# All norms of a two-block transformer kernel: split sums spread by two products, 16 columns inverted between block transposes

## The reference

```python
def rms_norm(x, g):
    xf = x.astype(jnp.float32)
    y = xf * lax.rsqrt(jnp.mean(xf * xf, axis=-1, keepdims=True) + NORM_EPS)
    return (y * g.astype(jnp.float32)).astype(x.dtype)
...
def first_block(...):
        xn = rms_norm(h, mix_norm[l])
        proj = jnp.einsum("bsd,dp->bsp", xn, w_in[l]) + b_in[l]
        ...
        hn = rms_norm(h, ffn_norm[l])
        ...
    return rms_norm(h, final_norm)
...
def hybrid_layer(x, norm_gain, w_in, w_out, rel_bias, cos, sin):
    hn = rms_norm_2(x, norm_gain)
    proj = hn @ w_in.astype(hn.dtype)
```

## Time and profile before

| | |
|---|---|
| median of three runs | 1179.32 us (1178.95 to 1179.41) |
| the profiled execution, its own time | 1178.76 us |
| its span | 1177.0 us |
| PE busy | 1169.8 us, 99% |
| DVE busy | 722.0 us, 61% |
| ACT busy | 538.1 us, 46% |
| POOL busy | 149.7 us, 13% |
| mean granted clock of PE | 0.998 |

### The profile page before, as it was taken

How to read it: one execution, slowest core, us unless ns; L and a number is a source line. 1 busy time by engine, 2 the same in 40 slices (tenths; PEclk the granted TensorE clock), 3 DMA queues, 4 the chain that set the end, 5 groups by cost and what they waited for, 6 DMA issues and landing times.

```text
span 1177.0 us, 15915 instructions
## 1 busy us (share of the span) xinstructions
PE 1169.8 (99%) x5704; PEld 964.7 (82%) x5704; DVE 722.0 (61%) x1230; ACT 538.1 (46%) x957; POOL 149.7 (13%) x143
## 2 busy tenths in 40 slices
PE   9999999999999999999999999999999999999997
PEld 8888888888888888888888887788888887788886
DVE  6655884564677777776752635866555445775554
ACT  5522671544444344443241434573664415664653
POOL 4000111002000000000010200256002121263000
PEclk9999999999999999999999999999999999999999
DMA  6333343233233233223323422453223443542221
GB/s 220 112 105 107 99 127 123 83 107 106 74 107 107 72 106 107 84 94 116 104 76 107 164 87 96 137 148 89 88 79 107 143 142 113 156 129 79 72 90 72
DMA packets 107594, 127.68 MB, mean 108 GB/s; under 512 B 6921, under 2 KB 85995, under 8 KB 107275
## 3 DMA queue, kind: packets, MB, share of 16 engines
q1 hardware_dynamic: 104859, 120.02, 31.9%
q10 hardware_dynamic: 2672, 6.82, 1.7%
HBM read 112.10 MB, written 2.14 MB: 97 GB/s over the span
## 4 chain that ended last, share of the span: by engine, by line
PE 99%; DVE 1%; ACT 0%; issue 0%; POOL 0%; POOLq 0%
PE main L717 24%; PE main L719 24%; PE main L718 24%; PE aux L719 3%; PE aux L718 3%; PE aux L717 3%; PE main L1052 2%; PE main L1054 2%; PE main L1053 2%; PE aux L806 2%; PE aux L793 1%; PE main L793 1%; PE main L1113 1%; PE main L1115 1%; PE main L1114 1%; PE aux L1006 1%
## 5 line engine op out<-in xcount | busy, mean ns | idle before, releaser
L717 PE MATMUL main<-x_hi,w_hi 128*128 128x512 f32 x980 | 387.3, 395 | 0.0
L718 PE MATMUL main<-x_lo,w_hi 128*128 128x512 f32 x980 | 381.9, 390 | 0.0
L719 PE MATMUL main<-x_hi,w_lo 128*128 128x512 f32 x980 | 381.8, 390 | 0.0
L1542 DVE TENSOR_TENSOR w_lo<-raw,w_hi 128x1024 fp32r<-128x1024 f32 x192 | 240.1, 1252 | 207.9 <-ACT w_hi L1157 203.1
L1157 ACT ACTIVATE w_hi<-raw 128x1024 fp32r<-128x1024 f32 x192 | 202.4, 1056 | 280.1 <-PE main L719 162.7
L717 PEld LDWEIGHTS main<-x_hi,w_hi 128*128 128x128 f32 x980 | 184.1, 188 | 42.1 <-issue 5.5
L719 PEld LDWEIGHTS main<-x_hi,w_lo 128*128 128x128 f32 x980 | 184.0, 188 | 38.9
L718 PEld LDWEIGHTS main<-x_lo,w_hi 128*128 128x128 f32 x980 | 184.1, 188 | 36.9 <-issue 0.2
L1196 ACT ACTIVATE soft_pair<-soft_pair,neg_peak 128x128 f32<-128x128 f32 (+2 forms) x96 | 50.2, 524 | 57.1 <-DVE neg_peak L1604 56.7
L2177 POOL COPY sum_sq<-squares 128x512 f32<-128x512 f32 x4 | 2.4, 611 | 455.9 <-ACT squares L1174 372.6
L2180 POOL TENSOR_TENSOR sum_sq<-sum_sq,squares 128x512 f32<-128x512 f32 x28 | 38.0, 1357 | 114.5 <-ACT squares L1174 113.7
(11 more groups left out here) (285 smaller groups left out, 1842.2 us busy)
## 6 DMA issues: line engine op xcount, KB each, us to landing
raw<-in_w_in_dram SPq DMA_DIRECT2D x96, 512.0 KB, 4.5
raw<-in_w_up_dram SPq DMA_DIRECT2D x44, 512.0 KB, 3.9
raw<-in_w_out_dram SPq DMA_DIRECT2D x24, 512.0 KB, 3.9
raw<-in_w_down_dram SPq DMA_DIRECT2D x22, 512.0 KB, 4.1
both_sums<-blocks_turned SPq DMA_DIRECT2D x72, 64.0 KB, 2.2
rel<-band_rows ACTq DMA_DIRECT2D x2, 2048.0 KB, 9.5
rel_part<-blocks_turned SPq DMA_DIRECT2D x48, 64.0 KB, 2.0
x_rows<-in_x_dram SPq DMA_DIRECT2D x4, 512.0 KB, 5.9
```

What stands on the lines that cost most here:

```text
L717: pe.matmul(bank, hi, right_hi[j], start=first and j == 0, stop=False)
L718: pe.matmul(bank, hi, right_lo[j], start=False, stop=False)
L719: done = pe.matmul(bank, lo, right_hi[j], start=False, stop=last and j == len(rows) - 1)
L1542: dve.tensor_tensor(w_lo[:, u % 4, :, :], raw_unit(u), w_hi[:, u % 4, :, :].bitcast(F32), ALU.subtract).then_inc(lo_ready, 1)
```

## The change

All four places are now done in one way, with one product pair for each norm:

- POOL rounds the finished sum into `sum_hi` (a cast to the rounded format) and subtracts it from the sum into `sum_lo`, which lies in the memory of `sum_sq` itself; it then raises `sum_split`. At the third place POOL also rounds the second sum into `gained_hi` (`second_rounded`), and DVE subtracts that one (`sum_split` again).
- PE multiplies both parts by `mean`, which now is in the rounded format, into `aux[3]` (and `aux[2]` for the second norm). PE waits for `sum_split` instead of `sq_added`. In the first norm the products stand two steps into unit 4 instead of ahead of it; in the second they stand where they stood; in the third and last they stand half way through value unit i == 2.
- DVE transposes the bank in blocks of 32x32, which leaves the 512 means in 16 columns (`turn_means`), adds the epsilon and inverts 16 or 32 columns; ACT takes the root of these (`root_ready`); DVE transposes them back as a broadcast into `factor` and, at the third place, `swapped_pair[:, 0, :]` (`spread_root`). `r_tok` is copied out of the 16 columns in four pieces (`factor_by_tokens`, `tokens_ready`).
- The column sums, the diagonals, their products and ACT's copies of 512 columns go, as does POOL's memset of `ones`.

```diff
-    mean = keep("mean", [P, P], F32)
-    ones = keep("ones", [P, P], F32R)
+    mean = keep("mean", [P, P], F32R)
+    r_cols = keep("r_cols", [P, 2, SEQ // 32], F32)
...
-        def sum_tokens(column, *squared):
-            for b in range(NB):
-                for j, tile in enumerate(squared):
-                    done = pe.matmul(aux[3][:, column + b:column + b + 1], tile[:, b * P:(b + 1) * P],
-                                     mean[:, 0:1], start=j == 0, stop=j == len(squared) - 1)
-            return done
-        def sum_norm(count, norms=1):
-            pe.wait_ge(sq_added, count)
-            if norms == 2:
-                pe.wait_ge(final_added, KT)
+        def sum_spread(splits, norms=1):
+            pe.wait_ge(sum_split, splits)
             for which in range(norms):
-                done = sum_tokens(NB * which, sum_sq[:, which, :])
+                upper = gained_hi[:] if which else sum_hi[:]
+                pe.matmul(aux[3 - which][:], mean[:], upper, start=True, stop=False)
+                done = pe.matmul(aux[3 - which][:], mean[:], sum_lo[:, which, :], start=False, stop=True)
             done.then_inc(norm_summed, 1)
-        def sum_spread(count):
-            pe.wait_ge(sq_added, count)
-            pe.matmul(aux[3][:], mean[:], sum_sq[:, 0, :], start=True, stop=True).then_inc(norm_summed, 1)
-        def spread_diagonal():
-            pe.matmul(aux[3][:], ones[:], diag_hi[:].rearrange("p b s -> p (b s)"),
-                      start=True, stop=False)
-            return pe.matmul(aux[3][:], ones[:], diag_lo[:].rearrange("p b s -> p (b s)"),
-                             start=False, stop=True)
-        def spread_factor(index):
-            pe.wait_ge(diagonal_ready, index - 1)
-            if index == 3:
-                pe.wait_ge(factor_ready, 3)
-            spread_diagonal().then_inc(factor_spread, 1)
...
+                if u == IN1 + FIRST_UNITS and k == 2:
+                    sum_spread(1)
...
-                    sum_spread(2 * KT)
+                    sum_spread(2)
...
+                        if i == 2 and k == pair[0]:
+                            sum_spread(4 + layer, 2 - layer)
...
-                if i == 1:
-                    sum_norm((3 + layer) * KT, 2 - layer)
-                if i == 3:
-                    spread_factor(2 + 2 * layer)
-                if i == 5 and layer == 0:
-                    spread_factor(3)
...
+        def factor_root(index, norms=1):
             act.wait_ge(norm_inverted, index + 1)
-            act.activation(r_tok[:, 0:norms, :], r_tok[:, 0:norms, :], ACT.Sqrt).then_inc(root_ready, 1)
-        def factor_root(index):
-            act.wait_ge(norm_inverted, index + 1)
-            act.activation(factor[:], factor[:], ACT.Sqrt).then_inc(factor_ready, 1)
-        def spread(index, target):
-            act.wait_ge(factor_spread, index - 1)
-            act.activation(target, aux[3][:], ACT.Copy).then_inc(factor_ready, 1)
+            act.activation(r_cols[:, 0:norms, :], r_cols[:, 0:norms, :], ACT.Sqrt).then_inc(root_ready, 1)
...
-                    act.wait_ge(root_ready, 1 + layer)
+                    act.wait_ge(tokens_ready, 1 + layer)
...
+                if i == 2:
+                    factor_root(2 + layer, 2 - layer)
...
+        def by_blocks(row):
+            return row.rearrange("p (b i) -> p b i", i=32)
+        def turn_means(row, bank):
+            steps.then(dve.transpose(by_blocks(row), by_blocks(bank[:])))
             steps.settle()
-            if two:
-                steps.then(dve.scalar_tensor_tensor(r_tok[:, 1, :], r_tok[:, 0, :], EPS2,
-                                                    aux[3][:, NB:2 * NB], ALU.mult, ALU.add))
-                steps.settle()
-            norms = slice(0, 2 if two else 1)
-            dve.reciprocal(r_tok[:, norms, :], r_tok[:, norms, :]).then_inc(norm_inverted, 1)
+            return by_blocks(row)[:, :, 0]
+        def spread_root(row, which):
+            return dve.transpose(by_blocks(row), r_cols[:, which, :].unsqueeze(2).to_broadcast((P, SEQ // 32, 32)))
         def invert_spread(index, eps):
             dve.wait_ge(norm_summed, index + 1)
-            steps.then(dve.tensor_scalar(factor[:], aux[3][:], eps, None, ALU.add))
+            means = turn_means(factor[:], aux[3])
+            steps.then(dve.tensor_scalar(r_cols[:, 0, :], means, eps, None, ALU.add))
             steps.settle()
-            dve.reciprocal(factor[:], factor[:]).then_inc(norm_inverted, 1)
-        def make_diagonal(which, ready=diagonal_ready):
-            for b in range(NB):
-                steps.then(dve.tensor_scalar(diag_hi[:, b, :], ident[:], r_tok[:, which, b:b + 1], None,
-                                             ALU.mult))
+            dve.reciprocal(r_cols[:, 0, :], r_cols[:, 0, :]).then_inc(norm_inverted, 1)
+        def invert_both():
+            dve.wait_ge(norm_summed, 3)
+            means = turn_means(factor[:], aux[3])
+            gained_means = turn_means(swapped_pair[:, 0, :], aux[2])
+            steps.then(dve.tensor_scalar(r_cols[:, 1, :], means, EPS1, None, ALU.add))
             steps.settle()
-            for b in range(NB):
-                done = dve.scalar_tensor_tensor(diag_lo[:, b, :], ident[:], r_tok[:, which, b:b + 1],
-                                                diag_hi[:, b, :].bitcast(F32), ALU.mult, ALU.subtract)
-            done.then_inc(ready, 1)
+            steps.then(dve.scalar_tensor_tensor(r_cols[:, 0, :], r_cols[:, 1, :], EPS2, gained_means,
+                                                ALU.mult, ALU.add))
+            steps.settle()
+            dve.reciprocal(r_cols[:], r_cols[:]).then_inc(norm_inverted, 1)
+        def factor_by_tokens(which):
+            for a in range(4):
+                rows = slice(32 * a, 32 * a + 32)
+                done = dve.tensor_copy(r_tok[rows, which, :],
+                                       r_cols[rows, 0, :].rearrange("p (b a) -> p b a", a=4)[:, :, a])
+            done.then_inc(tokens_ready, 1)
...
+        dve.wait_ge(root_ready, 1)
+        spread_root(factor[:], 0).then_inc(factor_ready, 1)
...
+                if i == 2:
+                    if layer:
+                        invert_spread(3, EPS2)
+                    else:
+                        invert_both()
+                    dve.wait_ge(root_ready, 3 + layer)
+                    factor_by_tokens(1 - layer)
+                    spread_root(factor[:], 0).then_inc(factor_ready, 1)
+                    if layer == 0:
+                        spread_root(swapped_pair[:, 0, :], 1).then_inc(factor_ready, 1)
                 if i < 31:
                     split(u + 4)
-                if i == 1:
-                    invert_norm(2 + layer, EPS2 if layer else EPS1, two=layer == 0)
-                    dve.wait_ge(root_ready, 1 + layer)
-                    make_diagonal(1 - layer)
-                if i == 4 and layer == 0:
-                    dve.wait_ge(factor_ready, 3)
-                    make_diagonal(0)
+                if i == 1 and layer == 0:
+                    dve.wait_ge(second_rounded, 1)
+                    dve.tensor_tensor(sum_lo[:, 1, :], sum_sq[:, 1, :], gained_hi[:].bitcast(F32), ALU.subtract)\
+                        .then_inc(sum_split, 1)
...
+            pool.wait_ge(sq_added, n0 + KT)
+            steps.then(pool.tensor_copy(sum_hi[:], sum_sq[:, 0, :]))
+            steps.settle()
+            pool.tensor_tensor(sum_lo[:, 0, :], sum_sq[:, 0, :], sum_hi[:].bitcast(F32), ALU.subtract)\
+                .then_inc(sum_split, 1)
...
+        pool.wait_ge(final_added, KT)
+        pool.tensor_copy(gained_hi[:], sum_sq[:, 1, :]).then_inc(second_rounded, 1)
```

More of the change, by code:

```diff
@@ L195, in two_blocks_kernel @@
     factor = keep("factor", [P, SEQ], F32)
-    diag_hi = keep("diag_hi", [P, NB, P], F32R)
+    sum_hi = keep("sum_hi", [P, SEQ], F32R)
     placed[0] = (placed[0] + K - 1) // K * K
@@ L199, in two_blocks_kernel @@
     sum_sq = keep("sum_sq", [P, 2, SEQ], F32)
-    diag_lo = nc.alloc_sbuf_tensor_at("diag_lo", [P, NB, P], F32R, offset=sum_sq_at + 4 * SEQ)
+    sum_lo = nc.alloc_sbuf_tensor_at("sum_lo", [P, 2, SEQ], F32R, offset=sum_sq_at)
     squares_at = placed[0]
@@ L277, in two_blocks_kernel @@
     straight_pair = at("straight_pair", [P, 2, SEQ], F32, 16)
+    gained_hi = at("gained_hi", [P, SEQ], F32R, 16)
     swapped_pair = at("swapped_pair", [P, 2, SEQ], F32, 76)
@@ L403, in two_blocks_kernel @@
     root_ready = sem("root_ready")
-    diagonal_ready = sem("diagonal_ready")
-    factor_spread = sem("factor_spread")
+    sum_split = sem("sum_split")
+    second_rounded = sem("second_rounded")
+    tokens_ready = sem("tokens_ready")
     factor_ready = sem("factor_ready")
@@ L825, in _ @@
         for _ in range(5):
-            pe.matmul(main[3][:, 0:P], mean[:], mean[:], start=True, stop=True)
+            pe.matmul(main[3][:, 0:P], mean[:].bitcast(F32), mean[:].bitcast(F32), start=True, stop=True)
```

(25 more changed lines are left out.)

4 lines of the change are left out of this document (1 added, 3 removed).

## The result

The changed kernel takes **1181.12 us** in the median of 19 runs (1179.6 to 1182.26); the kernel before, measured beside it, 1178.63 (19 runs, 1178.35 to 1179.41). The ratio is 1.0017, with a 95% interval from 1.0011 to 1.0024; the two medians alone differ by 2.49 us, 0.21%. So the loss is real, and it can't be told apart from the 0.2% (2.36 us) that the prediction took as its bound. The forecast was 1180.3, and no measurable change the likeliest outcome (0.54). One execution of all those reported here, the seventh of experiment 3, took 1980.04 us at a mean granted clock of 0.556, and nothing is read from it; without it that experiment's median is 1179.50 instead of 1179.53. The profiled execution of the changed kernel spans 1178.6 us, against 1177.0.

What follows compares the result with a forecast made beforehand. PE was taken as the bound, on the last chain for 99% of the span. Terms: -3.47 + 0.95 + 0.11 + 3.35 = +0.94 us, giving 1180.3 against the median 1179.32; 8 in 10: 1177.0 to 1183.0.

Steps and rivals of the forecast that it cites:

- PE's work: All four norms: 5.87 us of products removed from PE, 2.40 added in five pairs, net -3.47 us.
- Third norm's wait: Unit 118: PE waits 3.35 us for POOL's casts and subtraction, alternating with DVE's `w_lo`, then DVE's subtraction.
- Rival 2: All places: DVE and POOL don't hold each other up; 1177.2 us, chance 0.18.
- First norm's wait: Unit 4: PE waits 0.95 us for `sum_split`, including 0.23 for the weight load.
- Second norm: Second norm's pair: PE waits 0.11 us for the split sum, including 0.23 for the weights.
- Last norm: Last norm's pair: the split sum is ready at about 924.3, before PE asks at 928.7; no wait.
- Cast: POOL's rounding of the sums: taken to cost 0.61 us, like POOL's copy of the same shape.
- Rival 4: POOL's rounding: the cast costs as much as the subtraction, 1.30 us; 1182.9 us, chance 0.07.
- Rival 1, the clock: Third norm: PE's clock falls in a wait longer than 2.5 us, losing 2.4 us; 1182.7 us, chance 0.25.
- Value banks: Third and last norm: later `r_tok` hidden behind 24 products, counted nothing; without cover up to 3 us per layer.
- Inversions: First two norms: inversion steps shrink to transposes and 16 columns; readers several units from PE, counted nothing.
- Chances: Whole kernel against 0.2%, 1176.96 to 1181.68 us: faster 0.17, slower 0.29, rest 0.54.

Runs made afterwards that it cites:

- experiment 3: Changed kernel with thirteen unused products on PE ahead of the third norm's pair: 1179.53 us, ratio 1.0005 against the kernel before.
- experiment 6: Changed kernel with the first, third and last norms' pairs later and DVE's subtraction ahead of the three `w_lo`: 1174.92 us.
- Experiment 4: Changed kernel with DVE's subtraction for the third norm's second sum ahead of the three `w_lo`: 1176.44 us.
- experiment 2: Changed kernel with only the first norm's pair five steps later in its unit: 1180.43 us.
- experiment 5: Changed kernel with DVE's subtraction for the third norm's second sum behind two of the three `w_lo`: 1179.7 us.
- experiment 7: Changed kernel with the first norm's pair five steps later, the third and last norms' behind the second bank of value unit i == 3: 1177.71 us.
- experiment 8: experiment 6 with the first two norms inverted over all 512 columns, without transposes, as in the kernel before: 1176.77 us.

## Why the prediction was right, and where it wasn't

**PE's work** (-3.47): right. With waits and slow products taken out, the trace gives about -3.6 and experiment 6 between -3.7 and -4.0.

**Third norm's wait** (3.35): right in cause and nearly in size, 3.14. Every step of the alternation came out within 0.02; only the 0.23 added for the weight load was wrong. The pair's first product is recorded 0.05 us after the last input, and the load shows behind it: the first norm's second product starts 0.33 later instead of 0.23. Experiment 4 shows that the alternation, and not POOL's own work, makes the wait: alone POOL needs 2.5 us. Rival 2 falls, since it needed these 2.5 us beside DVE's `w_lo`, where POOL took 5.3. The Trainium skill, page "SBUF — State Buffer", section "SBUF: two separate sides", calls the shared pair an exclusive lock in which the later one "fully blocks"; by that rule the trace agrees (POOL's cast took 1.49 us among the `w_lo` and 0.61 alone).

**First norm's wait** (0.95): 0.74, with the pair's start-up 0.84; experiment 2 gives 0.88 in the medians. Cause shown, size 0.1 to 0.2 too high, for the same term. **Second norm** (0.11): none, for the same reason. **Last norm** (none): right.

**Cast** (0.61): right, 0.61 undisturbed. Rival 4 falls.

**Rival 1, the clock**: it had a chance of 0.25 beside the forecast, and it happened. Its size was wrong (1.6 us, not 2.4: the slow stretch was 3.4 us, not the 4.9 read near the start). So was its point of decision: a wait of 2.2 us brought it in experiment 5. The step that failed is the reading of the earlier trace rows, where I took the 2.5 us from PE's stop to the fall for the wait that is needed; experiment 5 shows a fall after PE had resumed. Nor are the 2.5 us a fixed length: behind PE's last product the clock fell after 2.35 to 5.01 us in the ten traces. And the argument against the rival, that PE was busy in full until the wait, did not keep the clock up; for that reason the likeliest case had put the term at nothing, and it measured 1.6.

**Why the total came so near**: partly by luck. The change was forecast at +0.94 and measured at +2.49. Without the clock's 1.6 it would have cost about +0.4, so a term left out of the likeliest case and terms 0.5 too high stood against each other. The forecast was also set on the median of three runs, 1179.32, where the kernel before measured 1178.63 beside the changed one. These 0.69 us, no part of the mechanism, brought 1180.3 to within 0.8 of 1181.12; on 1178.63 it would have been 1.55 off. The sum of the forecast's mechanism with rival 1 at its true price, 1178.63 + 0.4 + 1.6 = 1180.6, is 0.5 below the measured median.

**Value banks** (nothing): right, and the price without cover was right in kind: 1.76 and 0.64 in experiment 7, where "up to 3 us per layer" was a bound. **Inversions** (nothing): right for this change, where the kernel before, with wide inversions, has no such wait either. It isn't a property of the kernel, though: with the pair five steps later (experiment 8) they cost over 1 us. "Their readers are several units from PE" looked only at readers of the result, not at what stands behind the inversion in ACT's and DVE's queues.

**Chances**: the 0.29 for slower is too low by the prediction's own numbers, since rivals 1 and 4, both above 1181.68, make 0.32 without the edge of the forecast.

**Left open**: what the medians hold beyond the rows. Laid side by side with the kernel before, and counted from behind their starts, the traces put the changed kernel at +1.91 where the medians have +2.49. From it the medians step down by 4.87 in experiment 4, by 1.75 in experiment 5 and by 6.53 in experiment 6, the traces by 4.24, 0.84 and 5.60. The 0.6 of the changed kernel is in all three; up to 0.35 more, and the 0.7 us of experiment 8, stand in no row.

Open too is the changed kernel's wider scatter (2.7 us from lowest to highest, the kernel before's 1.1). One part is the start: the full clock came between 4.70 and 6.99 us in the ten traces, worth some 1.1 us if half of it is lost. Another is probably the fall: the kernels whose trace has a slow stretch scatter by 1.7 to 2.7 us, the others by 0.9 to 1.5. The mean granted clock of the changed kernel's runs is 0.997 or 0.998, but for one run at 0.999, which is also the fastest, 1179.6; by the estimate of experiment 5 the clock stayed up in it. The kernel before has runs from 0.998 to 1.000. But only one execution of each kernel was traced.

## What to carry to other kernels

A product whose input comes out of a chain over several engines should stand where that chain has ended, as long as PE has other products to put ahead of it: here two moved calls turned +2.5 us into -2.8, and a moved subtraction made it -4.0. When POOL and DVE both work from SBUF, write down their ends alternately, since what stands in DVE's queue sets POOL's pace. And price a wait of PE of two or three us, like these, twice: once for itself and once for the slow products that may follow (1.6 us here).

## What the hardware showed unexpectedly

PE's clock fell to 1.2 GHz after PE had already resumed at 2.4: in experiment 5 PE stood from about 671.7 to 673.7, was back at full speed, and was slow from 674.66 to 678.07; in experiment 2 it was back at 673.92 and slow from 674.80. The slow stretch was equally long in all three kernels that had one, 3.41 us, behind a wait of 3.14 as behind one of 2.22. The 1.76 us lost in experiment 7 were not followed by one.

The Trainium skill, page "TensorE: Matmul & The Clock Gate", section "HAM oscillation — how this bites in real kernels", has PE throttled in its waits for inputs, so that the next work starts cold. The trace of the changed kernel agrees (674.31 is ahead of the pair's start at 674.47); experiments 2 and 5 differ, since there the next work began warm and was slowed on its way.
